# Kept cache rows of a hybrid attention and retention step: their copies begun by ACT instead of the sync engine

## What is computed

```python
u = rms_norm(h, g_pre)
z = einsum('bsd,de->bse', u, w_in)        # w_in: 2048 x 22528, fp32
qa, ka, va, za, qr, kr, vr, zr, ga, gb = split(z)
# A: three dilated windows (128, 512, 2048 keys long), 8 heads of 128, mixed by their denominators
ya = combine_groups(outs, lses) * silu(za)
# B: chunkwise retention, 8 heads of 256 x 256 with a state per head
yr = norm(retention(qr, kr, vr, state)) * g_ret * silu(zr)
merged = sigmoid(ga) * (ya @ w_a_out) + sigmoid(gb) * (yr @ w_r_out)
h = h + rms_norm(merged @ w_o, g_post)
h = h + sigmoid(h @ w_ple_gate) * (p @ w_ple_proj)
# for the samples, each window's cache loses its oldest row and gains the new one:
new_win = concatenate([cache, new_kv], axis=1)[:, 1:]
```

## Time and profile before

| | us |
|---|---|
| three runs | 3046.01, 3043.8, 3042.0; median 3043.8 |
| profiled execution | 3037.74, its span 3035.8 |
| PE busy | 2911.3, 96% of the span |
| DVE busy | 1772.7, 58% |
| ACT busy | 1137.2, 37% |
| POOL busy | 362.2, 12% |
| granted TensorE clock, mean | 0.980 |

### The profile page before, as it was taken

The page is one execution under the profiler, slowest core; times in us unless marked ns, Lnnn a source line. Parts: engine busy times, 40 slices in busy tenths (PEclk is TensorE's granted clock), DMA queues, the critical chain, the costliest instruction groups (busy, mean ns, idle before and its releaser), DMA issues.

```text
span 3035.8 us, 57013 instructions
## 1 busy us (share of the span) xinstructions
PE 2911.3 (96%) x23406; PEld 2856.8 (94%) x23406; DVE 1772.7 (58%) x3159; ACT 1137.2 (37%) x2078; POOL 362.2 (12%) x537
## 2 busy tenths in 40 slices
PE   6899999999999999999999999999999999997898
PEld 6899999999999998989999999999999999997897
DVE  5557666676566666576676676665654433424532
ACT  6344343444444433333333333434343222323222
POOL 2000000000001002112112112110001100001211
PEclk8999999999999999999999999999999999998899
DMA  8555656656566454456465456476657665554353
GB/s 254 160 168 176 205 170 201 193 184 193 168 190 194 161 194 158 140 192 210 153 212 188 157 199 215 158 256 213 246 198 290 214 234 191 205 187 147 116 186 110
DMA packets 380307, 575.64 MB, mean 190 GB/s; under 512 B 16456, under 2 KB 340872, under 8 KB 376840
## 3 DMA queue, kind: packets, MB, share of 16 engines
q1 hardware_dynamic: 336448, 428.32, 41.1%
q0 software_dynamic: 43600, 143.69, 15.6%
HBM read 515.67 MB, written 232.42 MB: 246 GB/s over the span
## 4 chain that ended last, share of the span: by engine, by line
PE 82%; DMA 5%; DVE 5%; DVEq 3%; ACT 2%; issue 1%; ACTq 1%; SPq 0%; POOL 0%; POOLq 0%
PE acc L524 52%; PE acc L536 21%; DMA raw_weights<-in_w_in 1%; PE aux L756 1%; PE aux L767 1%; DVEq L1704 1%; DVE weights L1287 1%; PE aux L777 1%; DVE stage_buffers L1873 1%; ACT weights L933 1%; DMA y_scr<-stage_buffers 1%; PE aux L649 1%; PE aux L833 1%; DVEq L1392 1%; DMA stage_buffers<-in_x_prompt 1%
## 5 line engine op out<-in xcount | busy, mean ns | idle before, releaser
L524 PE MATMUL acc<-moving,weights 128*128 128x260 f32 x12384 | 1574.5, 285 | 7.5 <-DVE sampled L1368 7.5
L524 PEld LDWEIGHTS acc<-moving,weights 128*128 128x128 f32 x12384 | 1516.8, 189 | 16.9 <-issue 8.3
L1287 DVE TENSOR_TENSOR weights<-raw_weights,weights 128x512 fp32r<-128x512 f32 (+1 forms) x1030 | 697.8, 686 | 707.5 <-ACT weights L933 660.0
L933 ACT ACTIVATE weights<-raw_weights 128x512 fp32r<-128x512 f32 (+1 forms) x1030 | 634.1, 625 | 1185.5 <-PE acc L524 438.7
L536 PE MATMUL acc<-moving,weights 128*128 128x260 f32 x5760 | 711.2, 286 | 48.8 <-DVE moving L1843 20.5
L536 PEld LDWEIGHTS acc<-moving,weights 128*128 128x128 f32 x5760 | 705.3, 191 | 52.2 <-DVE weights L1287 22.3
L524 PE MATMUL acc<-combined_moving,weights 128*128 128x260 f32 x3096 | 430.2, 289 | 3.2 <-DVE partial_sums L1401 2.4
L524 PEld LDWEIGHTS acc<-combined_moving,weights 128*128 128x128 f32 x3096 | 394.9, 191 | 8.9 <-issue 5.9
L1368 DVE SCALAR_TENSOR_TENSOR stage_buffers<-acc,partial_sums 128x260 f32<-128x260 f32 x344 | 146.5, 478 | 165.8 <-PE acc L524 165.7
L933 ACT ACTIVATE weights<-combined_weights 128x512 fp32r<-128x512 f32 x172 | 108.1, 629 | 295.8 <-PE acc L524 279.7
L1287 DVE TENSOR_TENSOR weights<-combined_weights,weights 128x512 fp32r<-128x512 f32 x172 | 118.5, 689 | 145.8 <-ACT weights L933 145.0
(11 more groups left out here) (256 smaller groups left out, 1783.8 us busy)
## 6 DMA issues: line engine op xcount, KB each, us to landing
out<-in_cache_win SPq DMA_DIRECT2D x128, 1023.5 KB, 8.8
raw_weights<-in_w_in SPq DMA_DIRECT2D x96, 1024.0 KB, 6.2
raw_weights<-in_w_in SPq DMA_DIRECT2D x160, 512.0 KB, 5.3
out<-in_cache_win SPq DMA_DIRECT2D x32, 1022.0 KB, 10.9
out<-stage_buffers POOLq DMA_DIRECT2D x120, 256.0 KB, 3.3
stage_buffers<-in_cache_win POOLq DMA_DIRECT2D x48, 512.0 KB, 5.5
stage_buffers<-in_state_ret POOLq DMA_DIRECT2D x64, 256.0 KB, 3.7
raw_weights<-in_w_r_out SPq DMA_DIRECT2D x16, 1024.0 KB, 7.3
```

The costliest lines, as they stand in the source:

```text
L524: mm = pe.matmul(acc[:, m, half, 0:HC], W[:, g % AHEAD, wp, kk, :], mov(up, kk), start=(start and kk == 0 and n == 0), stop=(stop and kk = ...
L933: act.activation(W[:, g % AHEAD, 0, 0:src.shape[1]], src, ACT.Copy).then_inc(s_whi, 1)
L1287: dve.tensor_tensor(W[:, g % AHEAD, 1, 0:src.shape[1]], src, W[:, g % AHEAD, 0, 0:src.shape[1]].bitcast(F32), ALU.subtract).then_inc(s_wre ...
```

## The change

`keep_rows` is called by ACT instead of SP. In ACT's loop over the steps of a pair (`steps`) the copies of that pair stand behind the split `hi` of its step n = 1, and, where there are two, behind that of its last step. The counts per pair and the order of the copies are as before; `copies_of` holds the counts. SP keeps its loads and its wait at the end. Lines from 443 on move down by eight.

```diff
--- before.py
+++ after.py
@@ -440,6 +440,14 @@
                     src[at + ROW:at + ROW + n].rearrange("(p m n) -> p m n", p=16, n=inner)).then_inc(s_copy, 16)
     N_COPIES = NS * (16 + 4 + 1)
 
+    to_copy = iter([(g, b, c) for g in (2, 1, 0) for b in range(NS) for c in range((1, 4, 16)[g])])
+
+    def copies_of(q):
+
+        if q < RET:
+            return 2 if q % 5 in (0, 3) else 1
+        return 1 if q < GATE or WA <= q < WR or q >= WG else 2
+
     NEAR = [(b, kb) for kb in range(TB) for b in range(kb, min(kb + 2, TB))]
 
     def near_col(b, kb):
@@ -479,7 +487,6 @@
                 for m in range(2):
                     sp.dma_start(raw[:, half, :, m, :], rows[:, :, p.cols[m]:p.cols[m] + P]).then_inc(s_wload[half], 16)
 
-        to_copy = iter([(g, b, c) for g in (2, 1, 0) for b in range(NS) for c in range((1, 4, 16)[g])])
         for p in pairs:
             for half in halves_of(p):
                 load(p, half)
@@ -490,15 +497,6 @@
                 sp.wait_ge(s_stfree, H + 1)
                 for n in range(H):
                     sp.dma_start(X[:, n, 0:T], y_scr[n]).then_inc(s_yin[n], 16)
-            if q < RET:
-                copies = 2 if q % 5 in (0, 3) else 1
-            elif q < GATE or WA <= q < WR or q >= WG:
-                copies = 1
-            else:
-                copies = 2
-            for n in range(copies):
-                keep_rows(sp, *next(to_copy))
-        assert next(to_copy, None) is None
 
         sp.wait_ge(s_copy, 16 * N_COPIES)
 
@@ -1003,6 +1001,8 @@
                 for f in hooks.get(n, ()):
                     f()
                 hi(g + n + AHEAD)
+                if n in (1, p.n - 1)[:copies_of(p.nth)]:
+                    keep_rows(act, *next(to_copy))
 
         def scale_of(p):
             return RK ** -0.5 if RET <= p.nth < GATE and (p.nth - RET) % 4 == 1 else 1.0
@@ -1264,6 +1264,7 @@
             act.wait_ge(s_full[q], filled.due(f"sample out {q}"))
             a = act.activation(osr[0:NS, q, 0:T], aux[0:NS, q, :], ACT.Copy)
         a.then_inc(s_osrow, 1)
+        assert next(to_copy, None) is None
 
 
     @block.vector
```

## The result

The changed kernel takes 3093.86 us in the median of four runs (3084.63 to 3096.78), beside 3042.9 for the kernel before (3040.46 to 3046.01). The ratio is 1.0162, with a 95% interval of 1.0138 to 1.0185. The profiled execution took 3093.92 us, 56.2 us more than that of before. The forecast was 3042.4, in a range of 3030 to 3057.

What follows compares the result with a forecast made beforehand. It took PE as busy through attention, so a transfer costs time only where PE waits. +5 - 8 - 2 + 2.9 + 0.7 = -1.4 us: profiled 3036.3, 3042.4 us in the median of runs, range 3030 to 3057.

Steps and rivals of the forecast that it cites:

- attention: Attention stage: the next pair's half-1 load lands up to 2.43 us later, covered by six weight buffers, 8.7 us: 0.
- 2.43 us: On the DMA engines: one copy holds all sixteen for 2.43 us, with service roughly in order of arrival.
- Retention heads: Seven retention heads: a copy holds a load 2.43 us, lost whole in three: +5 us, bounds -3 and +17.
- the steady pairs of the output stages: Steady pairs of the output stages: the load's delay of 1.3 us is inside PE's lead, no loss.
- Start of the gates: Gate entry: y store and state loads freed of copies, wait and slow clock shrink: -8 us, bounds -9.2 and 0.
- Entry to the attention output: Attention-output entry: second pair's weights 2.4 us sooner, gate's store can lose 2.43 us: -2 us, bounds +1 and -8.
- ACT's issues: ACT's queue: the 168 copy issues fit into ACT's idle time: 0, bounds 0 and 34 us.
- the start-up: Start-up: ACT's first copy falls shortly before a table that DVE stands on: +0.7 us, bounds 0 and 2.43.
- the two entries with a load in the chain: Retention-output and PLE-gate entries: copy ahead of the load, 1.3 us each, +0.3 for the clock: +2.9 us.
- SP's relief: SP's queue: 168 issues, 119 us in all, leave SP, which waits for DVE's splits: worth nothing by itself.
- Copies in front of loads decide: Rival: copies delay each retention head's half-1 load, no gains at gates or attention output: +22 us, 3066; chance 0.11.
- Queues take turns: Rival: the y store never waited for copies, so both gains are 0, loads still lose: +8.6, 3052; chance 0.14.

Runs made afterwards that it cites:

- experiment 6: Changed kernel with a pair's copies behind steps 1 and 2 instead of 1 and the last: 3078.26 us, 1.0121 of the kernel before.
- experiment 2: Changed kernel with ACT beginning both copies of a pair behind step 5 of eleven-step pairs, step 2 of others: 3033.01 us, 0.9974 of the kernel before.
- experiment 3: Changed kernel with copies behind steps 7 and 8 of eleven-step pairs, 4 and 5 of eight, 3 of four: 3045.61 us, 1.0016.
- experiment 4: Changed kernel with each copy cut to 8 KB, the issues all kept: 3015.84 us, 0.9913 of the kernel before.
- experiment 5: Changed kernel with a pair's copies behind steps 2 and 3 instead of 1 and the last: 3057.06 us, 1.0046 of the kernel before.
- experiment 7: Changed kernel with both copies of a pair behind step 1, on ACT's queue: 3102.43 us, 1.0194 of the kernel before.
- experiment 1: Changed kernel with SP beginning the copies again, in front of the next pair's half-1 load: 3204.05 us, 1.0531 of the kernel before.
- experiment 8: As experiment 2, but 24 copies moved into attention from around the start of the gates and the attention output: 3018.92 us, 0.9916 of the kernel before.

## Why the prediction was wrong

**The step that failed is attention.** "Six weight buffers are ahead of PE, [...] That covers 2.43 us: 0." The larger error is the delay: in the median of attention's pairs the last landing of a half-1 load comes 9.45 us after its first issue, 5.85 before, which is 3.6 us and not 2.43, and the load shown above, with two copies in front, landed 14.25 us after its issue where the same load took 6.02 before, 8.2 us more. The forecast had counted one copy to a load; the second copy of a pair, at its last step, is begun some 3 us ahead of the next pair's load, so two loads of five have two in front. Of the 14 such loads of attention, 11 took 9.0 to 10.1 us, no longer than those with one in front, and three 13.1 to 14.3. PE lost 17.6 of the 22.2 us over the pairs around these three, and in experiment 6, with one copy in front, the same three took 9.3 to 10.2 us. The load shown, late as it was, met POOL's loads of cache rows. The queues from 363 to 369.3, its last part:

```profile
q1 hardware_dynamic: 1881, 0.95, 51.7%
q0 software_dynamic: 285, 1.04, 48.9%
```

POOL's queue (q0) moved as many bytes there as SP's. That this lengthened the load fits, but no run took POOL's loads away.

The cover was counted for the wrong work. The buffers cover late splits, and PE indeed never waited for one. They don't cover what stands behind the waiting sum on DVE. At the place shown PE began to wait, 1.10 us, with the load 8.2 us late, so the cover there was, by this estimate, some 7 us (not far below the forecast's 8.7) and was used up; and with the next load late too, DVE did not catch up, so that PE lost 6.8 us over this and the next two pairs. In experiment 6 a load that was 7.1 us late (12.9 for 5.8) cost PE nothing.

The prediction had described just this of a retention head ("DVE standing on it in order") and did not carry it over. It took the missing wait of PE in attention as a reason to leave the case out of the range; a row without a wait shows nothing of how much slack there is behind it.

**Retention heads: right mechanism, wrong size.** +23.0 for +5, beyond the bound of 17. From the fourth head on each pays at two pairs, not one, and half-1 loads land later by more than 2.43 us (the one of the earlier trace rows takes 14.85 us for 11.76, the median 11.8 for 7.4). Of the four heads that showed no wait of PE, three lost 4.2 to 4.9 us, so "a microsecond or two of slack" did not take it. And the added waits lowered the clock, which the forecast had at nothing here (37.5 us at 0.50 instead of 20.5).

**Entry to the output projection: no term.** That in "the steady pairs of the output stages the same 1.3 us is inside PE's lead" held: the five pairs of the retention output from its third on lost 0.0 us, with loads some 2 us longer. But the forecast had nothing for the first pairs of the output projection, +10.2 us. Their first load in the chain took 15.79 us, for 10.41 before and 11.6 with copies of 8 KB:

```profile
2631.36 15.79 DMA raw_weights<-in_w_o
```

One copy was begun 1.79 us ahead of it, another, begun 7.56 us ahead, had just landed, and POOL began ten loads of 260 KB between 2626.4 and 2631.7. With the one copy alone beside it (experiment 6) it took 14.6 us, and these pairs lost 4.3.

**Start of the gates: right sign, half the size.** PE waits 1.79 us at 2046.61 instead of 5.33, as forecast "below 2 us", and y stores land in 5.0 us in the median instead of 6.2. The granted clock stayed at 1.00 in the 2 us around that wait and was 0.89 over the next 16, where it had been 0.50 and 0.82:

```profile
2046.00:2048.00 2.00, 1.39 (x12) 1.39 (x13) 1.88 (x5) 0.00 (x0) 0.00 (x0) 1.00 1.02 164
2048.00:2064.00 16.00, 16.00 (x124) 16.00 (x123) 6.33 (x13) 4.88 (x8) 1.43 (x2) 0.89 0.73 264
```

The pair with this wait is 5.1 us shorter. But the half-1 loads around it now fly beside copies as well (one of 14.95 us, with copies begun 2.9 us ahead and 1.8 us behind, stands in the chain 28 us earlier), and with 1.2 us more in the pair before, 3.7 us are left of 8.

**Entry to the attention output: the bound came true**, +1.3 us for a bound of +1. The weights of the second pair landed after 9.34 us instead of 12.36, as forecast, but "ACT now begins two copies right there, around the gate's store" (3.8 us and 0.06 us ahead of it): that store took 9.99 us instead of 5.33, and PE waited 9.39 us instead of 5.3.

```profile
2362.52 9.99 DMA sg_scr<-stage_buffers
...
2376.25 0.71 DVE stage_buffers L1815
...
2377.09 2.94 PE acc L534 x12
```

**Right:** ACT's issues (0.52 us, no cost), the start-up (inside its bounds), and the two entries with a load in the chain (+2.2 for +2.9; the retention-output load 10.22 us instead of 9.07, the PLE-gate load 9.18 us instead of 7.88). At the second the size is luck: the working took a copy begun 1.1 us ahead of the load, and it was begun 3.2 us ahead, by which a block of 2.43 us would have cost nothing. SP's relief (worth nothing) was not measured by itself.

**The rivals.** 'Copies in front of loads decide' (0.11) was the nearest, but was priced without attention and the output projection, at 3066. 'Queues take turns' does not fit a stretch where almost only SP's and ACT's queues are busy. In experiment 2 SP issues the two DMAs of a load from 335.72 to 336.71, ACT two copies from 336.77. From 338.2 to 340.2 the packets moved are these:

```profile
q1 hardware_dynamic: 1239, 0.63, 109.0%
q0 software_dynamic: 30, 0.04, 6.2%
```

and from 340.2 to 343:

```profile
q10 hardware_dynamic: 24, 1.31, 113.6%
q1 hardware_dynamic: 295, 0.14, 17.9%
```

A copy's packets start 1.3 us after its issue where the engines are free (experiment 3: issued at 293.59, nothing on its queue but 4 small packets until 294.8). Here the first copy could by that have started at 338.1 and stood until 340.3, while the load's queue moved 1239 packets, 77 for each engine. The Trainium skill's rule ("DMA: Bandwidth & Descriptors", Queues, rings and completion order) has each engine take turns between the queues, and gives 64 descriptors as the most that one turn can hold; this stretch does not agree, if the copy was ready by 338.1, which no row shows.

Over attention and retention, a copy begun more than 1 us behind a load mostly leaves a load where it is in experiment 4 (1 to 2 us behind: 0.1 us later in the median of 25 loads), and one begun up to 2 us ahead makes it 3.2 to 3.6 us later (63 loads; changed kernel and experiments 2 and 3, loads with one copy near). But the order of arrival doesn't hold everywhere either. In experiment 5, with POOL's state loads in flight, a copy begun 1.04 us behind the load still made it 2 us later. In experiment 6 seven loads of attention with a copy level with them and a second begun 2.54 us behind took 12.3 to 12.9 us, where in the changed kernel, with the first copy alone, they took 8.7 to 10.7: there the later copy did get in. How the engines choose stays open, and so does why one copy costs a load 3.2 to 3.6 us and not its 2.43.

## What to carry to other kernels

When a transfer is moved, find the load that it will now fly beside, the instruction that waits for that load, and what stands behind this instruction on its engine: the slack is from the load's issue to that instruction, not the number of buffers ahead of the last consumer. A long copy that nothing waits for belongs behind the loads with the most slack and away from any stage where the bound engine waits for a transfer; moved there, it took this kernel 0.8% below its starting point, within 0.1% of a kernel that copies almost nothing. A trace without a wait tells that no time is lost there, not how much delay can be added.

## What the runs showed of the hardware

Copies begun close to the loads cost less from ACT's queue, 3102 us, than from SP's, 3204 (experiments 7 and 1), though the moments differ too. An issue of a copy on ACT took 0.52 us in the median and 0.64 at most in the changed kernel, beside 0.71 and 5.11 on SP, where the long ones stood behind loads; ACT is not free of long ones where it begins two copies in a row, up to 2.31 us in experiment 8. The fastest copy landed 5.1 us after its issue (experiment 5); of such a time 1.3 us pass before the first packet, and a packet of 64 KB takes 2.4 us at the fastest. A wait of 2.5 us in front of PE was followed by 3.3 us at half the clock.
